# Two attention schedules of a twelve-sublayer network: values behind later queries and keys in the mixed-family layers, a closed block left out of the selective layer

## The reference, cut to what matters

```python
# selective attention: 16 heads of 64; an index of 8 heads picks 64 keys for each query
visible = kpos[None, :] < ((qpos // CHUNK + 1) * CHUNK)[:, None]      # CHUNK = 64
score = einsum('bqh,bqhs->bqs', wi_b, relu(einsum('bqhd,bsd->bqhs', qi_b, ki)))
score = where(visible[None], score, -inf)
top_val, top_idx = lax.top_k(score, n_sel)                            # n_sel = 64
p = softmax(q_b . k[top_idx] * HEAD_DIM ** -0.5, masked where not valid)
out = p . v[top_idx]
```

## Time and profile before

| | us |
|---|---|
| median of 3 runs | 2387.6 |
| lowest, highest | 2386.41, 2393.24 |
| the profiled execution: its own time | 2389.38 |
| its span in the profile | 2387.6 |

### The profile page before, as it was taken

One profiled execution on the slowest core, in us unless ns is written; L12 is line 12 of the kernel. 1 busy time (PEld: TensorE's weight loads), 2 busy tenths in 40 slices (PEclk: granted clock), 3 DMA queues, 4 the chain that ended last, 5 costly groups with the idle time before them and its releaser, 6 DMA issues.

```text
span 2387.6 us, 55688 instructions
## 1 busy us (share of the span) xinstructions
PE 2251.9 (94%) x23028; PEld 2156.6 (90%) x23028; DVE 1568.9 (66%) x2402; ACT 1207.9 (51%) x2037; POOL 58.1 (2%) x83
## 2 busy tenths in 40 slices
PE   6899899999999989899988998999998999998998
PEld 5799799999999978799978998999897999887998
DVE  6854465566655688565588644655775777775776
ACT  5633454465544546454467334544675444675443
POOL 1000000000000010000010000000000000100000
PEclk8999999999999999999999999999999999998999
DMA  5310265533555433255523102555433554433653
GB/s 198 124 47 4 68 211 172 193 124 124 173 196 171 155 99 106 98 185 189 172 98 124 47 4 98 194 184 177 135 114 107 180 199 150 150 116 101 205 173 118
DMA packets 88437, 327.21 MB, mean 137 GB/s; under 512 B 9809, under 2 KB 9937, under 8 KB 87633
## 3 DMA queue, kind: packets, MB, share of 16 engines
q1 hardware_dynamic: 87984, 322.72, 40.2%
q0 software_dynamic: 288, 2.10, 0.3%
HBM read 323.73 MB, written 1.05 MB: 136 GB/s over the span
## 4 chain that ended last, share of the span: by engine, by line
PE 81%; DVE 10%; ACT 6%; issue 2%; ACTq 0%; DVEq 0%
PE bank L1931 15%; PE bank L1932 15%; PE bank L1933 15%; PE bank L1953 5%; PE bank L1954 5%; PE bank L1955 5%; DVE w_split L2135 2%; ACT w_split L2026 2%; PE bank L446 2%; PE bank L455 2%; PE bank L1353 1%; PE bank L1354 1%; PE bank L1355 1%; PE bank L469 1%; PE bank L1320 1%
## 5 line engine op out<-in xcount | busy, mean ns | idle before, releaser
L1931 PE MATMUL bank<-h_split,w_split 128*128 128x256 f32 x3176 | 912.2, 287 | 20.9 <-DVE h_split L2157 8.0
L1933 PE MATMUL bank<-h_split,w_split 128*128 128x256 f32 x3176 | 898.0, 283 | 0.0
L1932 PE MATMUL bank<-h_split,w_split 128*128 128x256 f32 x3176 | 897.9, 283 | 0.0
L2135 DVE TENSOR_TENSOR w_split<-ring_a,w_split 128x1024 fp32r<-128x1024 f32 x474 | 568.3, 1224 | 191.8 <-ACT w_split L2026 190.7
L1931 PEld LDWEIGHTS bank<-h_split,w_split 128*128 128x128 f32 x3176 | 602.4, 190 | 33.9 <-DVE h_split L2157 11.3
L1932 PEld LDWEIGHTS bank<-h_split,w_split 128*128 128x128 f32 x3176 | 598.3, 188 | 1.3
L1933 PEld LDWEIGHTS bank<-h_split,w_split 128*128 128x128 f32 x3176 | 597.0, 188 | 0.0
L2026 ACT ACTIVATE w_split<-ring_a 128x1024 fp32r<-128x1024 f32 x474 | 483.3, 1049 | 38.1 <-PE bank L1933 33.0
L1953 PE MATMUL bank<-act_split,d_split 128*128 128x256 f32 x1008 | 285.9, 284 | 3.8 <-DVE act_last L2218 2.4
L1954 PE MATMUL bank<-act_split,d_split 128*128 128x256 f32 x1008 | 285.5, 283 | 0.0
L1955 PE MATMUL bank<-act_split,d_split 128*128 128x256 f32 x1008 | 285.3, 283 | 0.0
(11 more groups left out here) (273 smaller groups left out, 3263.9 us busy)
## 6 DMA issues: line engine op xcount, KB each, us to landing
ring_a<-wa SPq DMA_DIRECT2D x474, 512.0 KB, 3.9
ring_d<-wd SPq DMA_DIRECT2D x132, 512.0 KB, 4.4
tab_sb<-tab SPq DMA_DIRECT2D x1, 2448.0 KB, 13.4
hT<-na POOLq DMA_DIRECT2D x2, 1024.0 KB, 5.3
xT<-x SPq DMA_DIRECT2D x1, 1024.0 KB, 4.9
out<-xT SPq DMA_DIRECT2D x1, 1024.0 KB, 3.9
vec_sb<-vec SPq DMA_DIRECT2D x1, 288.0 KB, 4.9
tab_sb<-tab SPq DMA_DIRECT2D x1, 65.0 KB, 4.7
```

The costliest lines, as they stand in the source:

```text
L1931: mm(dst, w[:, 0, ks], x[:, 0, k, :], start=(k == 0), stop=False)
L1932: mm(dst, w[:, 0, ks], x[:, 1, k, :], start=False, stop=False)
L1933: last = mm(dst, w[:, 1, ks], x[:, 0, k, :], start=False, stop=(k == KT - 1))
L2135: v.tensor_tensor(w_split[:, u % 4, 1, :], ring_a[:, u % 4, :], w_split[:, u % 4, 0, :].bitcast(f32), ALU.subtract).then_inc(s["w_lo"], 1)
```

## The change

In the **mixed-family** layers the units of the eight pairs come in another order: the values of a pair stand behind queries and keys of later pairs (v of pair 0 is unit 6, of pair t up to 5 unit 6 + 3t, those of pairs 6 and 7 are units 22 and 23). All steps from `scores` to `pv` come two slots sooner (LAG from 0 to -2, PV_AT from 10 to 8), the segments' norms one or two slots sooner, and the output units in slots 24 to 28 and 30 to 32. `norm_rope` of pair 0's q and k both stand in slot 2. `turn_v` comes one slot behind its unit, `copy_v` in the slot after that, and the unit of that slot waits for the copy: two slots behind the value's unit where it was three. The values of pairs 6 and 7 are turned together in slot 24. On VectorE `segment_low(1)` goes in front of `shifted`. The bank halves of `pv` and of the first segment's sum change places.

In the **selective** layer the closed block is left out: 384 columns instead of 512 in the index scores, their relu and sums, the scores, their bias and the copy of the turned block; `take_eight`, `exps` and `normed` work on 128 and 256 columns instead of twice 256; three transposes instead of four for a head; the second key tile enters `pv` for the second query tile alone; the maximum is taken by two instructions (128 and 256 columns) for a head instead of one. On VectorE `evac` goes ahead of `take_eight`, whose eight calls now stand once in each slot from 9 to 15 and once more in slot 10, and `out_low` goes ahead of `lo` and of the second `normed` of its slot.

```diff
-LAG = {"stick": 0, "dsa": 3, "multi": 0}
-PV_AT = {"stick": 8, "dsa": 13, "multi": 10}
+LAG = {"stick": 0, "dsa": 3, "multi": -2}
+PV_AT = {"stick": 8, "dsa": 13, "multi": 8}
-OUT_SLOTS = {..., "multi": (0, 1, 2, 4, 5, 6, 8, 9)}
+OUT_SLOTS = {..., "multi": (0, 1, 2, 3, 4, 6, 7, 8)}
+IN_TURN = [(role, t) for t in range(8) for role in range(3)]
+VALUES_LATE = [(0, 0), (1, 0), (0, 1), (1, 1), (0, 2), (1, 2), (2, 0), (0, 3), (1, 3), (2, 1), (0, 4), (1, 4), (2, 2),
+               (0, 5), (1, 5), (2, 3), (0, 6), (1, 6), (2, 4), (0, 7), (1, 7), (2, 5), (2, 6), (2, 7)]
+def unit_at(kind, role, t):
+    return FIRST[kind] + pair_units(kind).index((role, t))
+def norm_slot(kind, i):
+    return max(unit_at(kind, i % 2, i // 2) + 1, 2 if kind == "multi" else 0)
...
+        def keys_of(kind, qt):
+            if kind == "dsa":
+                return slice(0, P) if qt == 0 else slice(P, 3 * P)
+            return slice(qt * S, (qt + 1) * S)
...
# TensorE, before a unit
-                t = pair_at(L, n, 5)
-                if t is not None:
-                    pe.wait_ge(s["vtok_ready"], L["vt"] + t + 1)
+                for t in range(KT):
+                    if unit_at(kind, 2, t) + (2 if kind == "multi" else 3) == n:
+                        pe.wait_ge(s["vtok_ready"], L["vt"] + t + 1)
...
# TensorE, scores
-                        last = mm(B[e][:, qt * S:(qt + 1) * S], qkv[h, t, qt * P:(qt + 1) * P], qkv[h, 8 + t, :],
+                        keys = slice(0, (qt + 1) * P if kind == "dsa" else S)
+                        last = mm(B[e][:, keys_of(kind, qt)], qkv[h, t, qt * P:(qt + 1) * P], qkv[h, 8 + t, keys],
...
# TensorE, turn
+                if kind == "dsa":
+                    for b in range(3):
+                        last = nc.tensor.transpose(B[3][:, b * P:(b + 1) * P], p_[:, b * P:(b + 1) * P], T("ident"))
...
# TensorE, pv
+                        a = P if kind == "dsa" and st else 0
+                        last = mm(pv_bank(L, t)[h, a:S], v_pair(t)[:, st * P + HD * e:st * P + HD * e + HD],
+                                  turned(e)[:, st * S:(st + 1) * S - a], start=(st == 0), stop=(st == NT - 1),
...
# TensorE's list of a slot
-                if kind == "multi" and n in (17, 26):
-                    segment_sum(n // 9 - 1)
+                if kind == "multi" and n in (16, 24):
+                    segment_sum(n // 8 - 2)
-                t = pair_at(L, n, 3)
-                if t is not None:
-                    turn_v(t)
-                ... norm_rope(2 * t + 1) at 2, norm_rope(2 * t) at 1
+                for t in range(6 if kind == "multi" else KT):
+                    if unit_at(kind, 2, t) + 1 == n:
+                        turn_v(t)
+                if kind == "multi" and n == N:
+                    turn_last_v()
+                for i in range(NH):
+                    if norm_slot(kind, i) == n:
+                        norm_rope(i)
...
# ScalarE's list of a slot
+                for i in range(NH):
+                    if norm_slot(kind, i) + 1 == n:
+                        norm_rope_root(i)
+                for i in range(NH):
+                    if norm_slot(kind, i) == n:
+                        norm_rope_in(i)
+                for t in range(KT):
+                    if (N + 1 if kind == "multi" and t > 5 else unit_at(kind, 2, t) + 2) == n:
+                        copy_v(t)
...
# VectorE's list of a slot
                 t = pair_at(L, n, 8 + lag)
                 if t is not None:
                     normed(2 * t)
+                for i in range(NH):
+                    if norm_slot(kind, i) + 1 == n:
+                        norm_rope(i)
+                if kind == "multi" and n == 26:
+                    segment_low(1)
                 t = pair_at(L, n, 7 + lag)
                 if t is not None:
                     shifted(t)
+                t = pair_at(L, n, 11 + lag)
+                if t is not None and kind == "dsa":
+                    out_low(t)
...
                         lo(L, m)
                 t = pair_at(L, n, 8 + lag)
                 if t is not None:
                     normed(2 * t + 1)
-                t = pair_at(L, n, 11 + lag)
-                if t is not None and kind == "dsa":
-                    out_low(t)
...
+                if n < N:
+                    evac(n)
+                if kind == "dsa":
-                    if 9 <= n <= 14:
+                    if 9 <= n <= 15:
                         take_eight()
-                    if n in (10, 13):
+                    if n == 10:
                         take_eight()
...
-                if n < N:
-                    evac(n)
```

More of the change, by code:

```diff
@@ L1260, in index_pair @@
                         h = slice(HD * e, HD * e + HD)
-                        last = mm(B[e][:, qt * S:(qt + 1) * S], qkv[h, 24 + j, qt * P:(qt + 1) * P], qkv[h, 28, :],
-                                  start=True, stop=True)
+                        last = mm(B[e][:, keys_of(kind, qt)], qkv[h, 24 + j, qt * P:(qt + 1) * P],
+                                  qkv[h, 28, 0:(qt + 1) * P], start=True, stop=True)
                 last.then_inc(s["idx_mm"], 2)
@@ L1282, in turn_v, with turn_last_v @@
                 last.then_inc(s["vtok_done"], 1)
+            def turn_last_v():
+                pe.wait_ge(s["proj_evac"], L["proj"] + N)
+                for t in (6, 7):
+                    for st in range(NT):
+                        a = S * (t == 6) + st * P
+                        last = nc.tensor.transpose(B[6][:, a:a + P], qkv[:, 16 + t, st * P:(st + 1) * P], T("ident"))
+                last.then_inc(s["vtok_done"], 2)
             def scores(t):
@@ L1483, in copy_v @@
                 act.wait_ge(s["vtok_done"], L["vt"] + t + 1)
-                A(v_pair(t), B[6][:, S:2 * S], ACT.Copy).then_inc(s["vtok_ready"], 1)
+                half = slice(0, S) if kind == "multi" and t == 7 else slice(S, 2 * S)
+                A(v_pair(t), B[6][:, half], ACT.Copy).then_inc(s["vtok_ready"], 1)
             def exps(t, e):
@@ L1607, in att_act @@
                     index_high(2 * n - 9)
-                if kind == "multi" and n == 19:
+                if kind == "multi" and n == 18:
                     segment_high(0)
@@ L1705, in shifted @@
                     else:
-                        last = v.scalar_tensor_tensor(out=probs(t, e), in0=B[e][:, :], scalar=HD ** -0.5,
+                        w = 3 * P if kind == "dsa" else 2 * S
+                        last = v.scalar_tensor_tensor(out=probs(t, e)[:, 0:w], in0=B[e][:, 0:w], scalar=HD ** -0.5,
                                                       in1=bias(t, e), op0=ALU.mult, op1=ALU.add)
@@ L1711, in shifted @@
                     k = 4 * (t % 2) + 2 * e
-                    v.tensor_reduce(small[:, 48 + k:50 + k], probs(t, e).rearrange("p (a b) -> p a b", a=2),
-                                    AX.X, ALU.max, negate=True).then_inc(s["nmx_ready"], 1)
+                    if kind == "dsa":
+                        for qt in range(NT):
+                            last = v.tensor_reduce(small[:, 48 + k + qt:49 + k + qt],
+                                                   probs(t, e)[:, keys_of(kind, qt)], AX.X, ALU.max, negate=True)
+                    else:
+                        last = v.tensor_reduce(small[:, 48 + k:50 + k],
+                                               probs(t, e).rearrange("p (a b) -> p a b", a=2), AX.X, ALU.max,
+                                               negate=True)
+                    last.then_inc(s["nmx_ready"], 1)
             def normed(h):
@@ L1802, in att_dve @@
                     shifted(t)
-                if kind == "multi" and n in (18, 27):
-                    segment(n // 9 - 2)
-                if kind == "multi" and n == 28:
-                    segment_low(1)
+                t = pair_at(L, n, 11 + lag)
+                if t is not None and kind == "dsa":
+                    out_low(t)
+                if kind == "multi" and n in (17, 25):
+                    segment(n // 8 - 2)
                 for m in range(AHEAD + 1, N + KT):
@@ L2358, in constants @@
     vis = q[None, None, :] < (qq // CH + 1) * CH
-    put("visible", np.where(vis, 0.0, NEG).reshape(P, -1))
+    vis = np.where(vis, 0.0, NEG)
+    put("visible", np.concatenate([vis[:, 0, 0:P], vis[:, 1, :]], 1))
     delta = np.abs(q[None, None, :] - qq)
@@ L2388, in blocks, with in_pairs @@
     return w.reshape(KT, P, n, P).transpose(2, 1, 0, 3).reshape(n, P, KT * P)
-def in_pairs(b, order=range(KT)):
-    return np.stack([b[[t, KT + t, 2 * KT + t]] for t in order]).reshape(3 * KT, P, D)
+def in_pairs(b, kind, order=range(KT)):
+    return b[[KT * role + order[t] for role, t in pair_units(kind)]]
 def padded(w, n):
@@ L2409, in layout @@
         elif kind == "stick":
-            A += [in_pairs(blocks(I["sb_w_qkv"][0])), np.asarray(I["sb_w_out"][0]).reshape(KT, P, D)]
+            A += [in_pairs(blocks(I["sb_w_qkv"][0]), "stick"), np.asarray(I["sb_w_out"][0]).reshape(KT, P, D)]
```

86 lines of the change are left out of this document (32 added, 54 removed).

## The result

| | us |
|---|---|
| changed kernel, median of 4 runs | 2354.01 (2353.76 to 2355.06) |
| kernel before, median of 4 runs beside it | 2390.42 (2386.41 to 2394.53) |
| ratio | 0.9852, 95% interval 0.9832 to 0.9871 |
| profiled execution of the changed kernel: span, own time | 2353.3, 2355.06 |
| forecast | 2352.0 (2342.0 to 2367.0) |

The time falls by 36.4 us, or 33.6 against the median shown ahead. The three attention layers can be read by themselves. I take each from its mark, the last row in which TensorE, in the layer's first units, waits some 0.37 us for a part of `h_split`, to the first row in which it waits for a part of `h_split` in the next layer.

The account below looks back on a forecast made before the run. TensorE's waits, and its own work where it has none, were taken to bound the kernel. Selective layer 25.3 plus mixed-family layers 10.4 gave 35.7 us off the 2387.6 span, so a median of 2352, range 2342 to 2367.

Parts of the forecast that it names:

- Selective layer, sum 25.3: Selective layer: narrower work 5.3, `evac` ahead of `take_eight` 6.8 and `out_low` sooner 13.2 together gain 25.3 us.
- Narrower work: Selective layer: TensorE's narrower pair steps, transposes and `pv` save 6.0 us, 0.7 of it hidden in remaining waits: 5.3.
- `evac` ahead: Selective layer, slots 9 to 17: `evac` before `take_eight` cuts TensorE's lost pitch from 12.2 to 5.4 us, gain 6.8.
- Rival (c): Selective layer's struck-out stretch stays VectorE's: `evac` ahead brings 3, 2356 us; narrower instructions no cheaper either, 2362; chance 14%.
- `out_low` sooner: Selective layer: four waits before units go (7.8 us), waits at k5 and k6 shrink, k5 keeps its clock: gain 13.2.
- Mixed-family layer, 5.2: Each mixed-family layer: gains of 11.4 and 3.1 less losses of 1.1 and 8.2 leave 5.2 us, twice 10.4.
- Start: Mixed-family layer's start: both first norms in slot 2 gain 4.0 us, less 0.85 for the second norm's input: 3.1.
- The first turned head: Mixed-family layer's start: it comes too soon, its values behind five packed norms on VectorE; 1.1 us lost.
- The new wait: Mixed-family layer: units 8, 11, 14, 17, 20 and 23 wait for `copy_v`, costing 8.2 us together (4.2 to 14).
- Tail: Mixed-family layer's end: waits before k3 and k6 go and slow-clock units speed up, gain 11.4 us.
- rival (b): Mixed-family layers: new waits drop the clock or VectorE's backlog lasts; they gain nothing or lose 5 each, 2362 to 2372; 20%.
- At nothing: Host block order, shorter mask table, last two values turned in slot 24 and swapped bank halves were costed at zero.

Follow-up runs that it names:

- experiment 6: Changed kernel with the selective layer's `evac` and `out_low` orders and `take_eight` slots undone, so only the narrower width is new there: 2369.24 us, ratio 0.9897 to before.
- experiment 9: Changed kernel with, in mixed-family layers, pair 0's query norm back in slot 1 and `segment_low(1)` behind pair 7's `shifted`: 2359.45 us, ratio 0.9857 to before.
- experiment 8: Changed kernel with the selective layer's second `take_eight` of slot 10 moved to slot 15: 2361.1 us, ratio 0.9863 to before.

## Why the prediction came out right, and which steps didn't

**Selective layer, sum 25.3: 24.7.** Its stretches fit better than its parts. By the chain of experiment 6 the width brings 10.6 (5.3 forecast), `evac` with its slots 3.4 (6.8) and `out_low` 10.7 (13.2). 3.2 us of this were counted under the wrong name, as the second point shows; that the rest, 2.1 too little and 2.7 too much, cancels as well is luck.

- *Narrower work, 5.3.* TensorE's share was right: I had 2.8 + 1.8 + 1.4 less 0.7 hidden, and the runs give 3.8 + 1.6. The pair step of the scores is 0.86 instead of 1.06, the product of the values 0.80 instead of 1.01. What failed is the other engines' share, which this term put at nothing: 3.2 us of VectorE's and ScalarE's narrower calls come out in units 10 to 18, and in the tail the width brings 4.0 where TensorE has 1.2, the product 0.8, and 1.3 is a unit at full clock again (k6, 4.25 with all engines wide); most of the last 0.7 I put down to the softmax chain, whose wait before k6 is 2.94 instead of 2.65. Whether ScalarE's saving "lies beside other work" no run shows by itself.
- *`evac` ahead, 6.8.* The waits before norms went from 10.7 (five) to 2.4 (three) and two new ones came, much as drawn (those at the turned heads of slots 16 and 17 are 0.4 instead of 2.3). But the order alone is worth 3.4 to 3.9. My walk through the slots already had the narrow calls in it (1.43 instead of 1.69), so its 6.8 held both: 3.4 for the order and 3.2 for the width. (Its five waits add up to 5.5, not 5.4.) The number for the stretch was right, its name was wrong: from the mark to unit 19 the layer is 7.9 shorter, and the forecast has 6.8 plus 1.6 for TensorE's own narrower steps up to there. Rival (c) had the right size for the order, 3, and was wrong in having narrower calls bring nothing.
- *`out_low` sooner, 13.2: 10.7.* The four waits: 7.8 forecast, 7.1 measured. The tail: 5.4 forecast, 3.2 measured. The 1.4 us of clock "at k5" was not this part's: with the width alone k5 takes 2.95 already, and k6 is then the slow one (4.33); with `out_low` sooner k6 takes 2.95 too. At k5 a wait of 0.39 stays where I had none, and k0 has a new one of 0.63 in its middle, put down to a norm's last step on VectorE (L1696), which I had not seen.

The two pair steps, narrow and wide, in TensorE's timeline, the changed kernel first:

```profile
959.53 0.93 PE L1330 MATMUL bank<-qkv 64*128 64x128 f32 x8
960.39 0.39 PE L1391 MATMUL bank<-o_split,w_split 128*128 128x256 f32 x1
```

```profile
974.89 1.13 PE L1328 MATMUL bank<-qkv 64*128 64x256 f32 x8
975.95 0.44 PE L1353 MATMUL bank<-planes,qkv 128*64 128x256 f32 x2
```

A narrow pair in place of a wide one saves 1.06 - 0.86 = 0.20. In the index's four steps, where nothing waits, undoing TensorE's width costs 0.81 for four steps, the same 0.20 each. By an estimate from the Trainium skill, "TensorE: Matmul & The Clock Gate", section "LDWEIGHTS (loading the stationary operand)", four loads of 128/1.2 ns one behind the other would have held a narrow pair at 0.43 and left 0.11 a step. The measured 0.20 speaks against pricing the pair so.

**Mixed-family layer, 5.2: 4.6 and 5.3.** *Start* 3.1: 3.0 when it is undone (experiment 9), and 3.1 against the kernel before in the first layer. In the second it is 1.5 against the kernel before, because there the unit behind the same wait of 2.32 us already ran at full clock (rows at the end). *The first turned head*, 1.1: it loses 0.7, and not because the first norm moved, since it stands there with the norm in slot 1 as well. *The new wait* 8.2: 7.9. Term by term the lost pitch is 1.9 at unit 8 (2.2), 1.4 less 0.2 of transposes, so 1.2, at 11 and at 14 (1.15), 0.8 at 17 and 23 (0.7), 2.1 at 20 (2.3). *Tail* 11.4: no wait before k3 and k6, and the output's units take 2.88 to 3.06 each. By what the other terms leave it is 11.5 in the first layer and 12.3 in the second. I gave two reasons for k3, the segment's slot and its place ahead of `shifted`. The second does nothing in this schedule: in the changed kernel the low parts end at 1785.9 and k3 starts at 1788.83, and `shifted` takes 2.5.

**The clock**, rival (b), is in the result with one unit of the first mixed-family layer, and it was one of the signs named for being wrong; another slow unit, at 873.00, is in the selective layer, where the rival didn't have it. Unit 20 of the first mixed-family layer waits 1.83 us, as in the second. In the first it then takes 4.38 us (1755.88 to 1760.26, granted clock 0.64), in the second 3.03 (2102.09 to 2105.12, granted clock 1.00). Hence 149.2 against 147.8.

**At nothing** held: the host's order, the table and the swapped banks show nowhere, and the two pieces of the maximum take 0.27 and 0.41 us where one took 0.68.

## What to carry to other kernels

When several edits meet in one stretch, the walk that gives the stretch its number doesn't say which edit earned it: cost each edit with the others in place and once without them, and then look whether the sizes agree. Where an engine that is not the bound has a queue of its own, look in it for the step that waits for someone else: here `copy_v` needed nothing more from VectorE and stood behind a step that did, for 3.3 to 4.7 us a layer. And where a wait is the price of a schedule, look which buffer it is for: another half of another bank took it away whole, which no order of the queues did.

## What the runs showed of the hardware that was not expected

The same gap doesn't always give the same clock, but it does so in a pattern. The kernel before shows it at the start of its two mixed-family layers, in TensorE's timeline and in windows (columns as above):

```profile
1692.06 0.70 PE L1271 MATMUL bank<-dec,tab_sb 128*128 128x256 f32 x2 [2.32 <-ACT dec L1476]
...
2042.79 0.70 PE L1271 MATMUL bank<-dec,tab_sb 128*128 128x256 f32 x2 [2.32 <-ACT dec L1476]
...
1692.97:1697.44 4.47, 4.47 (x26) 4.38 (x25) 3.81 (x6) 2.65 (x5) 1.09 (x1) 0.65 0.46 149
2043.57:2046.64 3.07, 3.07 (x27) 3.04 (x26) 2.74 (x5) 2.34 (x6) 1.42 (x1) 1.00 0.30 96
```

The wait is the same, and the unit behind it takes 4.47 us in one layer and 3.07 in the other. In the changed kernel the wait of 1.83 us before unit 20 was followed by a unit of 4.4 us in the first mixed-family layer and of 3.03 in the second, and the length of the first layer, 149.2 to 149.3, came again in each of the seven other kernels that share its code, and so did that of the second, 147.8. With the layer's start 3 us later (experiment 9) unit 20 takes 3.03 in the first layer too. In the tail of the selective layer k6 stands behind a wait of 2.65 us in both kernels below, the changed kernel first, then the one of experiment 8; all waits from k0 on are alike to 0.01 us:

```profile
973.09 0.55 PE L1343 MATMUL bank<-tab_sb,planes 128*128 128x128 f32 x3 [2.65 <-DVE planes L1766]
973.51 0.36 PE L1391 MATMUL bank<-o_split,w_split 128*128 128x256 f32 x1
```

```profile
977.36 0.90 PE L1343 MATMUL bank<-tab_sb,planes 128*128 128x128 f32 x3 [2.65 <-DVE planes L1766]
977.91 0.56 PE L1391 MATMUL bank<-o_split,w_split 128*128 128x256 f32 x1
978.27 0.41 PE L1392 MATMUL bank<-o_split,w_split 128*128 128x256 f32 x1
```

One unit takes 2.95 us (granted clock 1.00) and the other 4.23 (0.66). So a term of clock of 1.3 to 1.5 us behind a wait of 2 us is neither safe to book as a gain nor as a loss; what decides it beyond the wait's length stays open.
